# Expert blocks of 160, 128, 96 and 64 places with 32-wide halves, in a mixed order of experts, the loop written out

## The chip, the core and the metric

One core of one Trainium2 chip runs the program. The metric is the device time in microseconds of one execution, from three executions of each kernel: here their median. The engines are TensorE (PE; its weight loads are listed apart as PEld), VectorE (DVE), ScalarE (ACT), GpSimd (POOL) and SyncE (SP), which issues most of the transfers. All compute engines run their instructions in the order of the program and wait on semaphores.

## What is computed

One decoder layer over 512 prompt tokens and 8 sample tokens: modulation, a first norm, a combined projection into three mixers (pooling, convolution, gated recurrence), an output projection, and then a mixture of experts. The change touches the mixture alone, cut here to its core (float32 throughout):

```python
logits = xt @ router_w + router_b                      # 520 tokens, 32 experts
top_v, top_i = lax.top_k(logits, 4); top_w = softmax(top_v)
# for each expert e, the rows of xt that chose it:
g = minimum(xblk @ w_gate[e] + b_gate[e], 7)
u = clip(xblk @ w_up[e] + b_up[e], -7, 7)
y = ((u + 1) * g * sigmoid(1.702 * g)) @ w_down[e] + b_down[e]
# each token: sum of its 4 rows y, weighted by top_w
```

Each of the three matrices of an expert is 1024 x 1024, 4 MB; the 32 experts hold 402.7 MB of weights, and each is read once. The tokens of these inputs fall on the experts unevenly: experts 0 and 1 get 85 and 46 rows, the other 30, sorted, get 146, 146, 120, 102, 101, 101, 90, 83, 66, 60, 60, and the rest 59 and fewer (counted from the reference's routing). 2080 rows in all.

## The kernel before

**Blocks.** Experts are handled in order of a rank: experts 0 and 1 have the ranks 0 and 1 whatever their load (their weights can be fetched before the routing is known), the others are ranked by load, computed on the device. A rank has a fixed number of places, in blocks of 64: two blocks for the ranks 0 and 1, three for 2 and 3, two for 4 to 11, one for 12 to 31, 46 blocks in all. Places that are not taken are skipped by the gathers and scatters, but are multiplied like the others. Rows beyond an expert's places go to `extras`, 24 optional passes after the loop; with these inputs none is taken, but PE still steps over them (17.2 us after its last product).

**Products.** A block of 64 rows is the stationary operand (128 x 64), the weights stream: `project` and `down` send, for each of the 8 pieces k of the contraction and each block, two matmuls (h = 0, 1) of 512 columns to the two halves of the array's columns; each float32 matmul is two MATMUL instructions in the trace, so there are 32 for one block and one matrix. `project(0, ...)` is the gate matrix, `project(1, ...)` the up matrix; both begin with a bias matmul per block (`btab`, `sel`, L1804). `turn_act` turns the activations of the blocks (four 128 x 128 transposes for each, L1499), `turn_rows` turns gathered rows (eight transposes).

**A stage `cycle(s, i)`** is on PE: gate and up of expert s, turns of rows for a coming expert, `down` of expert s - 1, `turn_act` of expert s. ACT evicts the gates (`gated`), the turned rows (`x_low`), the outputs of s - 1 (`y_rows`, L943) and then the turned activations aT of s (`a_turned`, L949); DVE clips (`clipped`), multiplies (`activate`), evicts the other half of turned rows (`x_high`, L1430) and makes `sel`. `down` of a stage waits for the aT of the stage before (`aT_a`), after gate and up are done.

**Order.** The first 11 stages (`PRE`) are written out: ranks 0, 1, 4, 2, 12, 13, 14, 3, 15, 16, 17; then `REP` = 7 rounds of a loop with three stages of 2, 1 and 1 blocks (`BLOCKS`, `RANKS`, `G_BANKS`, `TURNS` hold the tables).

**Weights.** SP fetches chunks of 1 MB into 18 buffers (`NBUF`); four chunks are one matrix, 384 chunks in all. Chunk n waits until PE has used chunk n - 18 (`m_used`). The first 12 are fetched before the routing is done. POOL issues the gathers of rows (`gather`) and the scatters of outputs (`scatter`), each after a copy of its 128 indices into a small tile (`index`, L611). `sunit` and `gidx` are the index tables that DVE makes just before the stage 0.

Of the kernel before, what the change touches and what calls it, by code (L numbers as in the profile page):

```python
# [28 lines left out]
COLS = 24 + XTRA  # L29
# [17 lines left out]
RANK_STEP = (1, 2, 2)  # L47
G_BANKS = ((0, 1), (4, 5), (4, 5), (4, 5, 0), (1,), (1,), (1,), (4, 5, 0), (1,), (1,), (1,), (4, 5), (1,), (1,))
U_BANKS = ((2, 3), (0, 1), (0, 1), (1, 2, 3), (2,), (2,), (2,), (1, 2, 3), (2,), (2,), (2,), (0, 1), (2,), (2,))
D_BANKS = ((2, 3), (2, 3), (4, 5), (3, 0, 4), (3,), (3,), (4,), (3, 0, 4), (3,), (3,), (3,), (4, 5), (3,), (3,))  # L50
Y_BUFS = ((0, 1), (2, 3), (4, 0), (1, 2, 3), (4,), (0,), (1,), (2, 3, 4), (0,), (1,), (2,), (3, 0), (1,), (2,))

TURNS = {-1: ((0, 0, 0),), 0: ((1, 1, 1),), 1: ((0, 0, 6),), 2: ((1, 1, 2), (0, 2, 3)), 3: ((1, 0, 14),),
         4: ((0, 1, 4), (1, 2, 5)), 5: ((0, 0, 15),), 6: (), 7: ((1, 1, 7),), 8: ((0, 0, 16),), 9: (), 10: ((0, 0, 17),),
         11: ((1, 1, 8),), 12: (), 13: ((0, 0, 18),)}
NEXT_COL = {(0, 0): 6, (0, 6): 3, (0, 3): 4, (0, 4): 15, (0, 15): 16, (0, 16): 17, (0, 17): 18, (0, 18): 19,
            (1, 1): 2, (1, 2): 14, (1, 14): 5, (1, 5): 7, (1, 7): 8, (1, 8): 9}
# [12 lines left out]
def trunk_program(nc, x_prompt, x_sample, state_pool, state_conv, state_lru_conv, state_lru_h, c_prompt, c_sample,  # L70
# [8 lines left out]
    def place(start, *items):  # L79
# [78 lines left out]
    (xc, yst_b), M1 = place(W0, ("xc", [P, KC, 64], F32), ("yst_b", [P, 2, 512], F32))  # L158
    (xrow, raw2, sel, gidx, sidx, sunit, gcur0, gcur1, scur0, scur1, scur2, scur3, scur4), M2 = place(
        N0, ("xrow", [P, 2, D], F32), ("raw2", [P, NBUF - 12, CH], F32), ("sel", [P, P], F32R),  # L160
        ("gidx", [P, COLS], I32), ("sidx", [P, COLS], I32), ("sunit", [P, COLS, 2], I32), ("gcur0", [P, 1], I32),
        ("gcur1", [P, 1], I32), ("scur0", [P, 1], I32), ("scur1", [P, 1], I32), ("scur2", [P, 1], I32),
        ("scur3", [P, 1], I32), ("scur4", [P, 1], I32))
    gcur, scur, xt = (gcur0, gcur1), (scur0, scur1, scur2, scur3, scur4), (xa, xb, xc)
# [17 lines left out]
    with ctx:  # L182
# [52 lines left out]
        y_a, cur_done, cur_set = sem("y_a"), sem("cur_done"), sem("cur_set")  # L235
# [57 lines left out]
        def val(c, k, i):  # L293

            return c if i is None else i * k + c

        def first_chunk(s):

            return 12 * s - 4 if s else 0

        def gate_end(s, i):
            return val(first_chunk(s) + 4, 36, i)

        def up_end(s, i):
            return val(first_chunk(s) + 8, 36, i)

        def down_end(s, i):

            return val(first_chunk(s) + 12, 36, i)

        def blocks(s, i, back=0):

            return val(sum(BLOCKS[:s - back]), 4, i)

        def turns(s, i):

            return val(1 + sum(len(TURNS[t]) for t in range(s)), 2, i)

        def y_uses(s, b):

            before = sum(Y_BUFS[t].count(b) for t in range(min(s, PRE)))
            return before
# [3 lines left out]

        def tasks(eng, cycle):

            for s in range(PRE):
                cycle(s, None)  # L330
            with eng.Fori(0, REP) as i:
                for s in range(PRE, PRE + 3):
                    cycle(s, i)
# [24 lines left out]
        def _(sp):  # L358
# [67 lines left out]
            def expert(s, i):  # L426

                if s < 2:
                    return s
                r = RANKS[s]  # L430
                at_ = slice(r, r + 1) if i is None else bass.ds(i * RANK_STEP[s - PRE] + r, 1)
                return sp.value_load(task_i[0:1, at_], min_val=0, max_val=E - 1)

            def fetch(s, i, c, src):

                n = first_chunk(s) + c
                if i is None and n < 12:
# [4 lines left out]
                elif i is None and n < NBUF:  # L442
                    sp.wait_ge(tables_done, 1)
                else:
                    sp.wait_ge(m_used, val(n - NBUF + 1, 36, i))
                m_load(n % NBUF, src)

            kept = [None]

            def cycle(s, i):  # L450

                if s == 2:
                    sp.wait_ge(tables_done, 1)
                e = expert(s, i)
                for c in range(8):
                    fetch(s, i, c, rows_of((moe_w_gate, moe_w_up)[c // 4], e, c % 4))
                if s:
                    if s == PRE:
                        before = sp.value_load(task_i[0:1, bass.ds(i * 2 + RANKS[PRE - 1], 1)], min_val=0, max_val=E - 1)
                    else:  # L460
                        before = kept[0]
                    for c in range(4):
                        fetch(s, i, 8 + c, rows_of(moe_w_down, before, c))
                kept[0] = e

            tasks(sp, cycle)
            e_last = sp.value_load(task_i[0:1, E - 1:E], min_val=0, max_val=E - 1)
            for c in range(4):
                n = first_chunk(E) + c
                sp.wait_ge(m_used, n - NBUF + 1)  # L470
                m_load(n % NBUF, rows_of(moe_w_down, e_last, c))
# [21 lines left out]
            for b in range(5):  # L493
                total = 16 * (y_uses(PRE - 1, b) + REP * sum(Y_BUFS[t].count(b) for t in (PRE - 1, PRE, PRE + 1)))
                sp.wait_ge(y_out[b], n * 16 + (total + 16 * (b == 2)) if b < 2 else total + 16 * (b == 2))
# [19 lines left out]
        def _(g):  # L515
# [89 lines left out]
            h2_last, y_last = g.to_reg(TOK - 1), g.to_reg(TOK * K * 2 - 1)  # L605
            copies = [0]

            def index(dst, src, i, per):

                copies[0] += 1  # L610
                g.tensor_copy(dst[:, :], src).then_inc(cur_done, 1)  # L611
                g.wait_ge(cur_done, val(copies[0], per, i))
                g.sem_inc(cur_set, 1)

            def gather(b, col, i, per=6):

                at_ = slice(col, col + 1) if i is None else bass.ds(i + col, 1)
                index(gcur[b], gidx[:, at_], i, per)
                g.indirect_dma_start(
                    out=xrow[:, b, :], out_offset=None, in_=h2_d,  # L620
                    in_offset=bass.IndirectOffsetOnAxis(ap=gcur[b][:, 0:1], axis=0),
                    bounds_check=h2_last, oob_is_err=False).then_inc(x_rows[b], 16)

            def scatter(b, unit, i, per=6):

                if i is None:
                    src = sunit[:, unit // 2, unit % 2:unit % 2 + 1]
                else:
                    src = sunit[:, bass.ds(i + unit // 2, 1), unit % 2]
                index(scur[b], src, i, per)  # L630
                g.indirect_dma_start(  # L631
                    out=y_d, out_offset=bass.IndirectOffsetOnAxis(ap=scur[b][:, 0:1], axis=0), in_=yst(b),
                    in_offset=None, bounds_check=y_last, oob_is_err=False).then_inc(y_out[b], 16)

            def scatter_all(s, i, before):

                first = (0, 2, 12, 4, 28, 29, 30, 8, 31, 32, 33, 14, 34, 35)[s]
                for b in range(BLOCKS[s]):
                    g.wait_ge(y_a, val(before + b + 1, 4, i))
                    scatter(Y_BUFS[s][b], first + b, i)  # L640

            def cycle(s, i):
                n = 1 + sum(len(TURNS[t]) for t in range(s))
                for b, _, col in TURNS[s]:
                    n += 1
                    g.wait_ge(xt_ps, val(n, 2, i))
                    gather(b, NEXT_COL[b, col], i)
                if s == PRE:
                    g.wait_ge(y_a, val(sum(BLOCKS[:PRE]), 4, i))
                    scatter(Y_BUFS[PRE - 1][0], 33, i)  # L650
                elif s:
                    scatter_all(s - 1, i, sum(BLOCKS[:s - 1]))

            g.wait_ge(tables_done, 1)
            gather(0, 0, None)
            gather(1, 1, None)
            g.wait_ge(xt_ps, 1)
            gather(0, 6, None)
            tasks(g, cycle)
            all_blocks, all_turns = sum(BLOCKS[:PRE]) + 4 * REP, 1 + sum(len(TURNS[t]) for t in range(PRE)) + 2 * REP  # L660
# [1295 lines left out]
```

## Time and profile before

| | us |
|---|---|
| three runs | 1493.52, 1494.40, 1495.11 |
| median | 1494.40 |
| the profiled execution's own time | 1492.49 |
| its span, first to last instruction | 1490.6 |
| before the first expert's gate matmul | 348.7 |
| the 32 experts, to the end of PE's last product | 348.7 to 1409.4 |
| optional passes stepped over, sum of rows, last norm | 1409.4 to 1490.6 |
| PE matmul busy in the span | 1346.0 (90%) |
| ACT, DVE, POOL busy | 203.9, 288.1, 131.8 |
| HBM read | 473.9 MB |

Start and length in the rows below are us from the start of the span; "x64" is the number of instructions merged into the row, and what stands in brackets is the idle time before it and what ended it. PE's matmuls overlap in its pipeline, so the distance between the starts of two rows is what a piece costs, not its length.

### The profile page before, as it was taken

What the parts mean: (1) busy time and instruction counts of PE and PEld (TensorE: products, weight loads), DVE (VectorE), ACT (ScalarE), POOL (GpSimd) and SP (SyncE); (2) the same over time, 40 slices, a digit from 0 to 9 for tenths busy, and PEclk for the clock granted to TensorE, in tenths of its full rate; (3) what the DMA queues carried; (4) which work ended last, traced back from release to release, by engine and by line L of the source; (5) the groups of instructions that cost most, each with busy time, mean ns of one, the idle gap of its engine ahead of it and who ended that gap; (6) DMA issues with size and microseconds to landing.
All of it is one profiled execution on the core that took longest, in us unless ns stands there. A gap on an engine that the chain in (4) does not pass through costs nothing.

```text
span 1490.6 us, 18893 instructions
## 1 busy us (share of the span) xinstructions
PE 1346.0 (90%) x7387; PEld 591.5 (40%) x7387; DVE 288.1 (19%) x539; ACT 203.9 (14%) x348; POOL 131.8 (9%) x247
## 2 busy tenths in 40 slices
PE   2999869757999999999999999999999999999756
PEld 1868748542333333333333333333333333333211
DVE  1633684560000010010001000010000001000026
ACT  3515432200010010000100110000100100001011
POOL 2010030000011011000100100001000000000100
PEclk7799979857999999999999999999999999999966
DMA  9441593459787599999999999999999999999753
GB/s 319 145 144 63 193 354 117 175 218 336 254 293 273 197 328 363 418 356 413 390 417 416 417 418 418 419 417 417 417 418 419 416 416 418 417 418 416 307 195 117
DMA packets 112644, 486.91 MB, mean 327 GB/s; under 512 B 14643, under 2 KB 22842, under 8 KB 79286
## 3 DMA queue, kind: packets, MB, share of 16 engines
q1 hardware_dynamic: 99690, 461.15, 79.1%
q0 software_dynamic: 9824, 21.78, 4.0%
q10 hardware_dynamic: 3076, 3.22, 0.7%
q8 instruction: 40, 0.66, 0.2%
q14 instruction: 14, 0.11, 0.0%
HBM read 473.93 MB, written 19.08 MB: 331 GB/s over the span
## 4 chain that ended last, share of the span: by engine, by line
PE 77%; DMA 9%; DVE 6%; SPq 3%; issue 2%; ACTq 1%; ACT 1%; POOL 0%; DVEq 0%; POOLq 0%
PE psum L1812 40%; PE psum L1826 18%; DMA raw<-in_moe_w_down 5%; PE psum L1499 4%; SPq L424 3%; PE psum L1494 2%; PE psum L1495 2%; PE psum L1496 2%; PE psum L1804 2%; DMA bd_x<-in_lru_wx 1%; PE psum L1648 1%; ACTq L705 1%; DMA raw<-in_w_out 1%; PE psum L1926 1%; DVE acc L1472 1%
## 5 line engine op out<-in xcount | busy, mean ns | idle before, releaser
L1812 PE MATMUL psum<-raw,xa 128*64 128x512 f32 x1536 | 341.4, 597 | 1.0 <-DMA raw<-in_moe_w_up 1.0
L1826 PE MATMUL psum<-raw,aT 128*64 128x512 f32 x1472 | 324.9, 595 | 7.1 <-DMA raw<-in_moe_w_down 6.3
L1812 PE MATMUL psum<-raw,xb 128*64 128x512 f32 x1280 | 284.5, 595 | 0.0
L1416 DVE TENSOR_SCALAR act_t<-psum 128x512 f32<-128x512 f32 x46 | 30.5, 689 | 961.8 <-PE psum L1812 961.8
L1812 PEld LDWEIGHTS psum<-raw,xa 128*64 128x64 f32 x1536 | 106.4, 137 | 208.7 <-issue 204.0
L1826 PEld LDWEIGHTS psum<-raw,aT 128*64 128x64 f32 x1472 | 103.6, 137 | 209.6 <-issue 189.3
L1812 PEld LDWEIGHTS psum<-raw,xb 128*64 128x64 f32 x1280 | 90.2, 137 | 179.4 <-issue 179.4
L929 ACT ACTIVATE glu<-psum 128x512 f32<-128x512 f32 x46 | 25.9, 596 | 309.0 <-PE psum L1812 309.0
L1494 PE MATMUL psum<-hT_hi,w_hi 128*128 128x260 f32 x208 | 59.4, 286 | 0.0
L1495 PE MATMUL psum<-hT_lo,w_hi 128*128 128x260 f32 x208 | 58.8, 283 | 0.0
L1496 PE MATMUL psum<-hT_hi,w_lo 128*128 128x260 f32 x208 | 58.6, 282 | 0.0
L611 POOL COPY gcur<-gidx 128x1 int32<-128x1 int32 (+1 forms) x28 | 8.0, 287 | 556.1 <-PE psum L1499 511.5
L943 ACT ACTIVATE yst_a<-psum 128x512 f32<-128x512 f32 x32 | 18.9, 596 | 205.2 <-PE psum L1826 205.2
L1499 PE MATMUL psum<-ident,xrow 128*128 128x128 f32 x208 | 30.9, 293 | 15.5 <-DMA xrow<-h_scratch,gcur 11.9
L611 POOL COPY scur<-sunit 128x1 int32 (+1 forms) x46 | 8.5, 184 | 410.0 <-ACT yst_b L943 209.0
L1555 PE MATMUL psum<-raw,cT 128*9 128x128 f32 x768 | 32.3, 334 | 10.8 <-DMA raw<-in_ada_w 9.0
L1804 PE MATMUL psum<-btab,sel 128*128 128x512 f32 x92 | 38.8, 471 | 0.9 <-DVE xa L1430 0.9
L1499 PEld LDWEIGHTS psum<-ident,xrow 128*128 128x128 f32 x208 | 25.8, 195 | 34.6 <-issue 22.6
L1494 PEld LDWEIGHTS psum<-hT_hi,w_hi 128*128 128x128 f32 x208 | 39.1, 188 | 0.9 <-issue 0.8
L1496 PEld LDWEIGHTS psum<-hT_hi,w_lo 128*128 128x128 f32 x208 | 39.3, 189 | 0.0
L1495 PEld LDWEIGHTS psum<-hT_lo,w_hi 128*128 128x128 f32 x208 | 39.1, 188 | 0.1
L631 POOL DMA_INDIRECT y_scratch<-yst_a,scur x33 | 33.5, 1014 | 26.5 <-POOL scur L611 26.5
(368 smaller groups left out, 1013.7 us busy)
## 6 DMA issues: line engine op xcount, KB each, us to landing
raw<-in_moe_w_gate SPq DMA_DIRECT2D x128, 1024.0 KB, 19.1
raw<-in_moe_w_up SPq DMA_DIRECT2D x128, 1024.0 KB, 22.1
raw<-in_moe_w_down SPq DMA_DIRECT2D x128, 1024.0 KB, 23.4
raw<-in_ada_w SPq DMA_DIRECT2D x24, 1024.0 KB, 9.1
yrow<-y_scratch SPq DMA_DIRECT2D x4, 2048.0 KB, 9.7
raw<-in_w_in SPq DMA_DIRECT2D x7, 1024.0 KB, 11.6
x<-in_x_prompt SPq DMA_DIRECT2D x2, 2048.0 KB
raw<-in_w_out SPq DMA_DIRECT2D x4, 1024.0 KB, 14.2
```

The lines of the kernel that those rows point to most:

```text
L424: sp.dma_start(buf(slot).rearrange("p (k n) -> p k n", k=2), src).then_inc(m_full[slot], 16)
L631: g.indirect_dma_start(out=y_d, out_offset=bass.IndirectOffsetOnAxis(ap=scur[b][:, 0:1], axis=0), in_=yst(b), in_offset=None, bounds_check ...
L929: ac.activation(glu[:, b, :], bk[bank], ACT.Gelu_apprx_sigmoid).then_inc(glu_done, 1)
L1416: v.tensor_scalar(act_t[:, b, :], bk[bank], 8.0, -6.0, ALU.min, ALU.max).then_inc(u_done, 1)
L1494: mm(out, lhi, rhi, start=start, stop=False)
L1495: mm(out, lhi, rlo, start=False, stop=False)
L1496: return mm(out, llo, rhi, start=False, stop=stop)
L1499: return nc.tensor.transpose(out, src, ident[0:rows, 0:rows])
L1555: last = mm(outs[j], cT[:, 4 * kh + k, :], raw[:, slot, 512 * k + P * j:512 * k + P * j + P], start=False, stop=(kh == 1 and k == 3))
L1804: mm(bk[bank], sel[:, :], btab[:, mat, :], start=True, stop=False)
L1812: last = mm(bk[bank][64 * h:64 * h + 64, :], x[:, 2 * j + kk, at_:at_ + 64], buf(slot)[:, w:w + 512], start=False, stop=(j == 3 and kk == 1))
L1826: last = mm(bk[bank][64 * h:64 * h + 64, :], aT[:, b, k % 4, 64 * (k // 4):64 * (k // 4) + 64], buf(slot)[:, w:w + 512], start=(k == 0), s ...
```

## The change

1. **Places.** Units of 32: rank 0 and 1 get 96 places, 2 and 3 get 160, 4 to 7 get 128, 8 to 12 get 96, the others 64 (`width_of` counts units of 32). That is 38 blocks of 64 and 9 of 32. With the loads above no expert overflows.
2. **Half blocks.** `products` gives a block of 32 rows four matmuls of 256 columns, one to each quarter of the array's columns; the output takes 256 columns of a bank, and its evictions on ACT and DVE are 128 x 256. Its bias is four float32 matmuls of 256 columns. It is turned by two transposes. Half blocks stand behind the full blocks of their expert within each k.
3. **Order.** `ORDER` mixes the ranks; all 32 stages are written out on every engine, no `Fori`. The order has runs of single blocks: two behind each expert of 128 places at first, then five stages of 96 in a row, later six single blocks (stages 22 to 27) between the two experts of 160.
4. **Banks.** New tables; the turned activations of a third block go to bank 4. PE now waits for `aT_a` (all turned activations so far evicted) at the top of each stage, ahead of the gate's bias; `down` no longer waits for it.
5. **Gathers and scatters.** `gather` takes only the rows needed (96, 32 or 128), straight from `gidx`; scatters read `sunit` or, for half blocks, the new table `qunit`. The copies of indices are gone from the 32 stages. There are 25 gathers and turns of rows where there were 28 and 26; no stage has two turns (two had). `sunit` and `qunit` are made behind `tables_done` (4 and 8 small operations of DVE), no longer ahead of it.

```diff
-BLOCKS = (2, 2, 2, 3, 1, 1, 1, 3, 1, 1, 1, 2, 1, 1)
-RANKS = (0, 1, 4, 2, 12, 13, 14, 3, 15, 16, 17, 5, 18, 19)
-PRE, REP = 11, 7
+ORDER = (0, 1, 13, 14, 4, 15, 16, 5, 17, 18, 6, 8, 9, 10, 11, 12, 7, 19, 20, 21, 22, 2, 23, 24, 25, 26, 27, 28, 3, 29, 30, 31)
+def width_of(rank):
+    return 2 + (rank < 13) + (rank < 8) + (rank < 4) - 2 * (rank < 2)
+BLOCKS = {2: (64,), 3: (64, 32), 4: (64, 64), 5: (64, 64, 32)}
+G_BANKS = {2: (0,), 3: (0, 1), 4: (0, 1), 5: (0, 1, 3)}
+U_BANKS = {2: (1,), 3: (5, 4), 4: (4, 5), 5: (4, 5, 2)}
+T_BANKS = (6, 7, 4)
...
-    index(gcur[b], gidx[:, at_], i, per)
-    g.indirect_dma_start(
-        out=xrow[:, b, :], out_offset=None, in_=h2_d,
+def gather(n):
+    col, rows, _ = GATHERS[n]
+    rows_from(xrow[0:rows, n % 2, :], gidx[0:rows, col:col + 1], rows, x_rows[n % 2])
...
 for h in range(2):
     for a in range(2):
-        link(v.tensor_scalar(sunit[...], ...))          # ahead of tables_done
+        link(v.tensor_scalar(sunit[...], ...))          # behind tables_done
+for a in range(2):
+    for q in range(4):
+        link(v.tensor_scalar(qunit[32 * q:32 * q + 32, :, a], idx_f[64 * a:64 * a + 32, 0:15], 4.0, float(q),
...
+def bias(out, mat, w):
+    if w == 64:
+        mm(out, sel[:, :], btab[:, mat, :], start=True, stop=False)
+    else:
+        for g4 in range(4):
+            h, c = g4 // 2, 256 * (g4 % 2)
+            mm(out[32 * g4:32 * g4 + 32, :], sel[:, 64 * h:64 * h + 32].bitcast(F32),
+               btab[:, mat, c:c + 256].bitcast(F32), start=True, stop=False)
+def products(out, w, x, k, weights, start, stop):
+    for g4 in range(128 // w):
+        last = mm(out[w * g4:w * g4 + w, :], x[g4], weights[:, 8 * w * g4:8 * w * g4 + 8 * w],
+                  start=start, stop=stop)
...
 pe.wait_ge(xg_d, ...)
+if s:
+    pe.wait_ge(aT_a, before)
 project(0, ...)
...
-    pe.wait_ge(aT_a, val(before, 4, i))
     down(...)
```

How it stands on PE inside the gate matrix of an expert of more than two blocks. Before, rank 2 (`raw_164` is the second group of weight buffers, xb and xc the turned rows of its blocks 1, 2 and 3):

```order
L1812 MATMUL psum<-raw_164,xb 64x512 [waits m_full14]
L1812 MATMUL psum<-raw_164,xb 64x512 x3
L1812 MATMUL psum<-raw_164,xc 64x512 x2
L1812 MATMUL psum<-raw_164,xb 64x512 x4
L1812 MATMUL psum<-raw_164,xc 64x512 x2
```

And in the changed kernel, in the first stage (rank 0, one block of 64 and one of 32):

```order
L1812 MATMUL psum<-raw,xb 64x512 [waits m_full0]
L1812 MATMUL psum<-raw,xb 64x512
L1812 MATMUL psum<-raw,xb 32x256 x4
L1812 MATMUL psum<-raw,xb 64x512 x2
L1812 MATMUL psum<-raw,xb 32x256 x4
```

Before, all products have the one shape 64x512; now the shape goes from 64x512 to 32x256 and back at each k of the stages with a half block.

On PE at the border between two stages, where the turned activations of one expert are followed by the bias of the next; before:

```order
L1499 MATMUL psum<-ident,act_t 128x128 [waits xg_d,xg_a,act_done]
L1499 MATMUL psum<-ident,act_t 128x128 x11
L1804 MATMUL psum<-btab,sel 128x512 [waits xg_d,y_a,xg_a,sel_done]
L1812 MATMUL psum<-raw,xa 64x512 [waits m_full8]
```

and now, behind rank 2 as before:

```order
L1497 MATMUL psum<-ident,act_t 128x128 [waits xg_d,xg_a,act_done]
L1497 MATMUL psum<-ident,act_t 128x128 x9
L1802 MATMUL psum<-btab,sel 128x512 [waits aT_a,xg_d,y_a,xg_a,sel_done]
L1812 MATMUL psum<-raw,xa 64x512 [waits m_full8]
```

The bias has one semaphore more, `aT_a`, and there are 10 transposes where there were 12.

## Rows read from the trace of the kernel before

**Rows 1.** The page: GB/s that the DMA engines moved, 40 slices of 37.3 us.

```profile
GB/s 319 145 144 63 193 354 117 175 218 336 254 293 273 197 328 363 418 356 413 390 417 416 417 418 418 419 417 417 417 418 419 416 416 418 417 418 416 307 195 117
```

**Rows 2.** Windows: us, busy time of PE, PEld, DVE, ACT, POOL, clock, DMA share, GB/s.

```profile
757.78:1119.50 361.72, 361.72 (x1698) 126.98 (x1697) 27.51 (x52) 31.18 (x57) 30.84 (x48) 1.00 1.02 418
1119.50:1409.50 290.00, 281.81 (x1307) 97.20 (x1305) 20.64 (x39) 24.33 (x44) 24.33 (x38) 1.00 0.99 404
```

**Rows 3.** Waits of PE, 330 to 1435 us: total us, times, longest us.

```profile
PE psum L1826 <- DMA raw<-in_moe_w_down: 6.3, 10, 1.3
PE psum L1499 <- DVE xb L1430: 6.0, 3, 2.4
```

**Rows 4.** The chain of waits: one-block stages and the starts of the loop's last rounds.

```profile
1029.81 13.88 PE psum L1812 x64
...
1120.25 13.88 PE psum L1812 x64
...
1148.69 1.09 PE psum L1499 x8
...
1158.06 7.02 PE psum L1812 x32
...
1213.38 13.88 PE psum L1812 x64
```

**Rows 5.** The chain of waits over the whole span: the end.

```profile
1307.00 13.88 PE psum L1812 x64
...
1409.45 17.23 issue
```

**Rows 6.** Timeline of PE: a stage border of two-block experts.

```profile
414.79 13.95 PE L1826 MATMUL psum<-raw,aT 128*64 128x512 f32 x64
428.67 1.09 PE L1499 MATMUL psum<-ident,act_t 128*128 128x128 f32 x8
429.52 0.72 PE L1804 MATMUL psum<-btab,sel 128*128 128x512 f32 x2
430.17 13.95 PE L1812 MATMUL psum<-raw,xa 128*64 128x512 f32 x64
```

**Rows 7.** Timeline of PE: two steps k apart in the three-block expert.

```profile
480.59 1.03 PE L1812 MATMUL psum<-raw,xc 128*64 128x512 f32 x4
...
483.16 1.03 PE L1812 MATMUL psum<-raw,xc 128*64 128x512 f32 x4
```

**Rows 8.** Timeline of PE: the sample rows' output projection, four column groups of 256.

```profile
272.55 0.62 PE L1727 MATMUL psum<-w_hi,oS 128*8 128x256 f32 x8
...
279.02 0.61 PE L1727 MATMUL psum<-w_lo,oS 128*8 128x256 f32 x8
279.57 0.63 PE L1750 MATMUL psum<-rw,h2T 128*128 128x32 f32 x4
```

**Rows 9.** Windows over those groups (columns as in rows 2).

```profile
272.55:279.02 6.47, 6.47 (x121) 3.30 (x124) 3.01 (x4) 2.95 (x7) 0.53 (x1) 1.00 0.21 84
```

**Rows 10.** Timeline of all engines at a border between single blocks.

```profile
1029.10 0.71 PE L1804 MATMUL psum<-btab,sel 128*128 128x512 f32 x2
1029.38 0.60 ACT L949 ACTIVATE aT<-psum 128x512 f32<-128x512 f32 x1
```

**Rows 11.** Timeline: ACT at the border of rows 6.

```profile
429.76 1.09 ACT L949 ACTIVATE aT<-psum 128x512 f32<-128x512 f32 x2
```

**Rows 12.** Timeline: the last aT eviction and the product that waits for it.

```profile
1399.86 0.60 ACT L949 ACTIVATE aT<-psum 128x512 f32<-128x512 f32 x1
...
1400.55 3.65 PE L1826 MATMUL psum<-raw,aT 128*64 128x512 f32 x16 [0.73 <-ACT aT L949]
```

**Rows 13.** Timeline: from the tables to the first gather.

```profile
333.67 0.84 DVE L1398 TENSOR_SCALAR sunit<-idx_f 64x48 int32<-64x48 f32 x4
...
334.79 0.31 POOL L611 COPY gcur<-gidx 128x1 int32<-128x1 int32 x1 [44.54 <-DVE gidx L1403]
336.01 1.09 POOL L619 DMA_INDIRECT xrow<-h_scratch,gcur  x1 [0.92 <-POOL gcur L611]
```

More of the change, by code:

```diff
@@ new lines, in plan_turns @@
+def plan_turns():
+    made, turns = set(), [[] for _ in range(E + 1)]
+    for s, r in enumerate(ORDER):
+        col = unit_of(r) // 2
+        if col not in made:
+            made.add(col)
+            rows = {2: P, 3: 96, 4: P, 5: P}[WIDTH[s]]
+            turns[s].append((col, rows, 0 if WIDTH[s] == 2 else 1))
+        if WIDTH[s] == 5:
+            turns[s - 1].append((col + 1, 32, 2))
+    flat = [(s - 1, t) for s in range(E + 1) for t in turns[s]]
+    return [[(n,) + t for n, (c, t) in enumerate(flat) if c == s - 1] for s in range(E + 1)], [t for _, t in flat]
@@ L291, in buf, with gate_end, up_end, down_end @@
             return raw[:, n, :] if n < 12 else raw2[:, n - 12, :]
-        def val(c, k, i):
-            return c if i is None else i * k + c
         def first_chunk(s):
             return 12 * s - 4 if s else 0
[L301 to L322, printed above, removed]
+        def gate_end(s):
+            return first_chunk(s) + 4
+        def up_end(s):
+            return first_chunk(s) + 8
+        def down_end(s):
+            return first_chunk(s) + 12
+        def bank_of(banks, s, b):
+            w = BLOCKS[WIDTH[s]][b]
+            return bk[banks[WIDTH[s]][b]][:, 0:8 * w]
+        def down_bank(s, b):
+            w = BLOCKS[WIDTH[s]][b]
+            banks = D_EARLY if s < E - 1 and WIDTH[s + 1] == 5 else D_BANKS[WIDTH[s]]
+            return bk[banks[b]][:, 0:8 * w]
+        def y_uses(b):
+            return len(range(b, ALL_BLOCKS, Y_BUFS))
         def yst(b):
             return yst_a[:, b, :] if b < 3 else yst_b[:, b - 3, :]
[L327 to L333, printed above, removed]
         def extras(eng, cycle):
@@ new lines, in _, with index @@
+            g.wait_ge(tables_done, 1)
+            gather(0)
+            gather(1)
+            g.wait_ge(xt_ps, 1)
+            gather(2)
+            g.wait_ge(units_done, 1)
+            for s in range(E):
+                for n, _, _, _ in TURNS[s + 1]:
+                    g.wait_ge(xt_ps, n + 1)
+                    if n + 2 < ALL_TURNS:
+                        gather(n + 2)
+                if s:
+                    scatter(s - 1)
+            scatter(E - 1)
+            def index(dst, src, at_, q):
@@ L624, in scatter @@
[L624 to L660, printed above, removed]
[L661 to L664 removed]
             def extra(q):
[L668 to L670 removed]
+                g.wait_ge(xt_ps, q + ALL_TURNS)
@@ new lines, in a_turned @@
+            def a_turned(blocks, before, q=None):
+                for b, w in enumerate(blocks):
+                    act.wait_ge(at_ps, before + b + 1 if q is None else q * 2 + (before + b + 1))
+                    ac.activation(aT[:, b, 0:w // 16, :].rearrange("p a b -> p (a b)"), bk[T_BANKS[b]][:, 0:8 * w], ACT.Copy)\
+                        .then_inc(aT_a, 1)
+            act.wait_ge(tables_done, 1)
+            x_low(xb, GATHERS[0][1], 1)
+            for s in range(E):
+                gated(gate_end(s), [bank_of(G_BANKS, s, b) for b in range(len(BLOCKS[WIDTH[s]]))])
+                for n, _, rows, x in TURNS[s + 1]:
+                    x_low(xt[x], rows, n + 1)
+                if s:
+                    y_rows(s - 1)
+                a_turned(BLOCKS[WIDTH[s]], blocks_before(s))
@@ L1797, in turn_rows, with project @@
                 for k in range(KC):
-                    last = turn(bk[6 + k // 4][:, (k % 4) * P:(k % 4) * P + P], xrow[:, b, k:D:KC], P)
+                    last = turn(bk[6 + k // 4][:, (k % 4) * P:(k % 4) * P + rows], xrow[0:rows, b, k:D:KC], rows)
                 last.then_inc(xt_ps, 1)
-            def project(mat, banks, parts, slot0, full):
-                for bank in banks:
-                    mm(bk[bank], sel[:, :], btab[:, mat, :], start=True, stop=False)
+            def bias(out, mat, w):
+                if w == 64:
+                    mm(out, sel[:, :], btab[:, mat, :], start=True, stop=False)
+                else:
+                    for g4 in range(4):
[6 more added lines that the diff above has]
+                              start=start, stop=stop)
+                return last
+            def project(mat, outs, widths, parts, slot0, full):
+                for out, w in zip(outs, widths):
+                    bias(out, mat, w)
                 for j in range(4):
@@ L1808, in project, with down @@
                     for kk in range(2):
-                        for bank, (x, at_) in zip(banks, parts):
-                            for h in range(2):
-                                w = D * kk + 512 * h
-                                last = mm(bk[bank][64 * h:64 * h + 64, :], x[:, 2 * j + kk, at_:at_ + 64],
-                                          buf(slot)[:, w:w + 512], start=False, stop=(j == 3 and kk == 1))
+                        for out, w, (x, at_) in zip(outs, widths, parts):
+                            last = products(out, w, [x[:, 2 * j + kk, at_:at_ + w]] * 4, 2 * j + kk,
+                                            buf(slot)[:, D * kk:D * kk + D], False, j == 3 and kk == 1)
                     last.then_inc(m_used, 1)
-            def down(banks, slot0, full):
+            def down(outs, widths, slot0, full):
                 for j in range(4):
@@ L1857, in cycle @@
                 if s >= 3:
-                    pe.wait_ge(y_a, blocks(s, i, 2))
-                project(0, G_BANKS[s], parts_of(s), c0, full(0))
+                    pe.wait_ge(y_a, blocks_before(s - 2))
+                project(0, [bank_of(G_BANKS, s, b) for b in range(len(widths))], widths, parts_of(s), c0, full_at(c0))
                 if s >= 2:
-                    pe.wait_ge(y_a, blocks(s, i, 1))
-                project(1, U_BANKS[s], parts_of(s), c0 + 4, full(4))
-                n = 1 + sum(len(TURNS[t]) for t in range(s))
@@ L1864, in cycle @@
-                for b, _, _ in TURNS[s]:
-                    rows[0][b] += 1
-                    turn_rows(b, val(16 * rows[0][b], 16, i), val(before, 4, i) if before else None, val(n, 2, i))
-                    n += 1
-                if s:
-                    pe.wait_ge(glu_done, val(before + BLOCKS[s], 4, i))
-                    pe.wait_ge(aT_a, val(before, 4, i))
-                    down(D_BANKS[s - 1], c0 + 8, full(8))
-                pe.wait_ge(act_done, val(before + BLOCKS[s], 4, i))
@@ new lines, in _ @@
+                for n, _, rows, _ in TURNS[s + 1]:
+                    turn_rows(n % 2, rows, 16 * (n // 2 + 1), before if before else None, n)
+                if s:
+                    pe.wait_ge(glu_done, before + len(widths))
+                    down([down_bank(s - 1, b) for b in range(len(BLOCKS[WIDTH[s - 1]]))], BLOCKS[WIDTH[s - 1]],
+                         c0 + 8, full_at(c0 + 8))
+                pe.wait_ge(act_done, before + len(widths))
+                pe.wait_ge(xg_a, turns_before(s + 1))
@@ L1883, in _ @@
+                pe.wait_ge(xg_d, turns_before(s + 1))
+                turn_act(widths)
+            pe.wait_ge(y_a, ALL_BLOCKS - 1)
+            pe.wait_ge(aT_a, ALL_BLOCKS)
             c0 = first_chunk(E)
-            down((3,), c0, lambda j: 16 * ((c0 + j) // NBUF + 1))
+            down([down_bank(E - 1, 0)], (64,), c0, full_at(c0))
             def extra(q):
```

338 lines of the change are left out of this document (152 added, 186 removed).

## The prediction

> **What bounds the kernel now.** I read the expert part, 348.7 to 1409.4 us, in the windows first. From 758 to 1120 us PE is busy for all of 361.7 us at the full clock, and the DMA share is 1.02 at 418 GB/s [rows 2]: both look full, so the busy shares don't decide. The chain of waits does: three rounds of the loop start 90.44 us apart (1029.81, 1120.25) and consist of PE work alone, then the distance grows to 93.13 and 93.62 us [rows 4, 5], with waits for chunks of `down` [rows 3]. So PE sets the pace almost to the end, and the fetches run ahead of it by up to 18 chunks. That lead is spent only in the last quarter: 36 chunks of 1.05 MB in 90.44 us are already 417 GB/s, and rows and outputs come on top. Earlier, the bandwidth is not used (175 to 363 GB/s in slices 8 to 16 [rows 1]), because experts of two and three blocks hold the buffers. A better order can win back only what PE lost to chunks. I put that at 2.7 + 3.2 us for the two long rounds and 5.2 us at the end: from 1307.00, one undisturbed round less its last turn and bias (1.1), plus the last `down` (7.0) and its wait for aT (0.9), ends at 1404.2 instead of 1409.4. In all **11.1 us**. Everything else must come out of PE's own work.
>
> **The change on PE, part by part.** The unit: one block and one matrix cost 7.02 us alone (L1812 x32) [rows 4] and two cost 13.88 [rows 6]; three blocks repeat a step k every 2.57 us [rows 7], 0.858 for each. So one block more is 6.87 us for a matrix, 20.6 us for three.
> - 46 full blocks become 38: 8 x 20.6 = **-164.9**.
> - 9 half blocks make 9 x 24 = 216 steps. Their form, four column groups of 256 float32 columns, stands in the trace: 15 groups of eight instructions from 272.55 to 279.02, 0.431 us each, at the full clock [rows 8, 9]. It is half a full block's 0.858, so four groups do run side by side. 216 x 0.431 = **+93.1**.
> - The shape changes twice in each of these steps. What a change costs: a `down` of 32 pairs needs 16 x 0.858 = 13.73 us, but its successor starts 13.88 behind it [rows 6]: 0.15 for one leaving and one entering, of which the starts of the single instructions give 0.10 to the pipe that runs empty and 0.05 to the weight load that was not pulled ahead. Behind the four-group stream it is 279.57 - 279.02 - 0.43 = 0.12 [rows 8]. Leaving 64-wide 0.10, entering 32-wide 0.03 (between 0.01 and 0.05, by columns loaded), leaving 32-wide 0.12, entering 64-wide 0.05: 0.29 a step, 0.27 to 0.32. 216 x 0.292 = **+63.1** (58 to 69). No row shows 64 to 32; every other change of width between busy stretches of this trace (128 to 64 and back, 128 to 32 and back; rows 6 and 8 stand for them) costs it, and I take the same.
> - Biases: 16 of 0.32 go ((430.17 - 429.52) / 2 [rows 6]), 18 of half blocks come at 0.43 + 0.12 + 0.02: -5.1 + 10.2 = **+5.1**.
> - Turns: 14 transposes of 0.109 less, -1.5; one turn of rows less, -1.1 (L1499 x8) [rows 4]. Two of the three waits for DVE behind a second turn go, -3.6 of the 6.0 [rows 3]; the first, of stage 0, stays. **-6.2**.
>
> Without the new wait that is -9.8: the half blocks save nearly nothing, since a step of 0.723 us replaces one of 0.858.
>
> **The new wait.** `aT_a` now stands ahead of the gate's bias, and PE has nothing behind it that may pass: gate and up of the next expert (14 us or more) queue there. Between single blocks the bias starts at 1029.10 and the aT eviction ends at 1029.98 [rows 10]: 0.88 us of new idle time. Between two-block experts the bias starts at 429.52 and ACT ends at 430.85, since it first evicts two outputs: 1.33 [rows 6, 11]. All of it was hidden under the gate. In the new order 12 of the 31 borders are single behind single (0.88), 6 are larger experts behind single or nothing (0.94), 7 follow a 96 (1.10), 4 follow a 128 (1.29), 2 follow a 160 (1.54): 32.2 us. From ACT's end to PE's start it takes 0.09 more (1400.46 to 1400.55 [rows 12]), 2.8. **+35.0**; the ends are 31 x 0.97 = 30 and 31 x 1.42 = 44. I take the composition, as each class has its row or lies between two.
>
> **Start.** Four `sunit` operations (0.84) leave the path and so does the index copy (1.22 from 334.79 to 336.01) [rows 13]: **-2.0**; the gather of 96 rows lands as that of 128 did. The rest of POOL's changes is hidden: gathers are issued two turns ahead, over 40 us. The end from 1409 on stays, with the 17.2 us of stepping [rows 5].
>
> **Chunks.** PE's sum so far is +23.2, so PE is slower and the fetches, which need 1 MB / 418 GB/s = 2.51 us a chunk, wait for it more than before. Single blocks drain the lead: 12 chunks (30.1) and their share of the 2080 rows of 8 KB (0.5 MB, 1.3) are 31.4 us of fetching, against 23.3 of PE (3 x 7.02, two biases, four transposes, 1.0 of border) or 24.4 with a turn. In the run of six singles, the first of which has the `down` of an expert of 160, that is five times 7.5, or 38 of the lead's 45 us (18 chunks); before it, experts of 96 and 128 fill it up. So the 11.1 us of waits go: **-11.1**.
>
> **Sum.** -164.9 + 93.1 + 63.1 + 5.1 - 6.2 + 35.0 - 2.0 - 11.1 = **+12.1**. The profiled execution took 1492.49 us (1.9 below the median of the three), and would take 1504.6; the median goes from 1494.4 to **1506.5**.
>
> **A rule against the rows.** The rows show empty-pipe gaps only where 128 is one of the two widths. The Trainium skill (TensorEngine Tiling (Array Packing), Key Properties) says that a change of tiling mode, not of the tile, drains TensorE, and lists 64 and 32 columns as different modes; by that rule the +63.1 stands. Its page TensorE: Matmul & The Clock Gate (Part 3, The mechanism) speaks against the change altogether: a weight load overlaps running matmuls only where its row group differs, and here all four column groups share their rows. Rows 9 speak against that for this form: 124 loads, busy 3.30 us, lie inside 6.47 us in which PE is busy throughout.
>
> **Rivals.**
> 1. *No drain between 64 and 32.* Both are column groups, and only leaving them might empty the pipe. Then the 63.1 and 2.2 of the biases go: -53 against before. The fetches become the bound in the runs of singles and give back 3 to 10, so about **1448** (1444 to 1456). For: no row shows this pair. Against: every other pair pays. Chance 0.15.
> 2. *The lead runs dry.* In the six singles the margin is 7 us at 418 GB/s. At the 404 of the last window [rows 2] a single costs 1.1 us more, and the lead may not be full behind the 160. Then 5 to 15 us of chunk waits stay: **1517** (1512 to 1524). This decides from about 9 us of shortfall a single. Chance 0.08.
> 3. *Weight loads are not hidden in the half blocks.* With 32 columns loaded in place of 8, 3.30 / 15 = 0.22 us a step would come bare: +47, **1554**. It is what the second rule above would make of rows 9. Chance 0.03.
> 4. *Smaller prices.* If the border waits sit at their low end (-5) and a fifth to a third of the drains is covered by the loads (-12 to -21), the time is 1480 to 1490. Chance 0.07.
>
> **How the numbers follow.** My forecast, all terms as priced, has 0.67; its own range from the bounds of drains, waits and biases is 1497 to 1516. With rival 2, the upper part of rival 4 and half-hits between them, 1488 to 1522 holds 8 in 10; the case without drains is left out below. A measurement of this kernel can tell 0.2% (3 us) from no change. Faster by more: rival 1, and most of 4, 0.20. Within: 0.04. Slower: 0.76.
>
> **What will show it.** In the changed trace: (a) 32x256 products in groups of eight 0.43 us long, and the next 64-wide start about 0.55 after the group's first, a step of 96 places taking 1.58 us (1.29 if nothing drains); (b) a new PE wait for ACT's aT at the bias, 31 times, near 1.0 us each; (c) chunk waits near nothing; (d) a single's stage 23.3 us without a turn; (e) the last product ending near 1421. The forecast is wrong if (a) shows 1.29, or if (b) is missing.

## The result, and the profile after

The changed kernel takes 1505.82 us (median of four runs, 1503.76 to 1508.16) against 1494.14 us (four runs, 1493.52 to 1495.11): a ratio of 1.009 with a 95% interval of 1.0066 to 1.0114, 11.7 us slower. Forecast were 1506.5 us and +12.1 us.

The page of the changed kernel (its profiled execution took 1508.16 us, the slowest of the four): busy time of TensorE and of its weight loads, and the DMA row in GB/s that answers to [rows 1].

```profile
span 1506.4 us, 20098 instructions
...
PE 1334.8 (89%) x8453; PEld 549.9 (37%) x8453; DVE 284.3 (19%) x548; ACT 199.1 (13%) x350; POOL 111.7 (7%) x171
...
GB/s 321 146 136 49 204 338 124 168 226 354 275 360 417 416 419 416 399 410 406 371 299 312 304 306 311 301 413 416 418 416 394 404 416 416 417 419 416 302 167 116
```

TensorE is busy 11 us less (it was 1346.0) in a span 16 us longer. The fetches reach full bandwidth in slice 13 and not in slice 17, some 145 us earlier, but in slices 21 to 26, the five experts of 96 places, they fall to 300 GB/s, since TensorE frees the buffers too slowly there: such a stage takes 42.9 us (753.99 to 796.92), in which 12 chunks are 293 GB/s, and rows and outputs come on top. Where it stands idle, in the waits of TensorE from 330 to 1440 us (total us, times, longest):

```profile
PE psum L1802 <- ACT aT L960: 32.8, 31, 1.6
PE psum L1497 <- DMA xrow<-h_scratch,gidx: 10.8, 1, 10.8
PE psum L1497 <- DVE xb L1436: 1.8, 1, 1.8
...
```

The first row is the new wait, once at each of the 31 borders; the two rows left out are 0.7 us each. No wait for a chunk is left, where [rows 3] had 6.3 us for `down` alone. One matrix with a full and a half block, and the biases around it, in the timeline of TensorE (start, length; L1806 is the half block's bias):

```profile
753.99 0.47 PE L1802 MATMUL psum<-btab,sel 128*128 128x512 f32 x1 [1.35 <-ACT aT L960]
754.38 0.64 PE L1806 MATMUL psum<-btab,sel 128*32 128x256 f32 x8
754.95 12.70 PE L1812 MATMUL psum<-raw,xb 128*64 128x512 f32 x96
767.58 0.50 PE L1802 MATMUL psum<-btab,sel 128*128 128x512 f32 x1
```

From 754.95 to 767.58 are 12.63 us for eight steps, 1.58 us a step. Two full blocks took 13.88 us [rows 6], one takes 7.02 [rows 4]. So a block of half the rows costs 5.61 us of the 6.87 of a full one. In an expert of 160 places the timeline shows the two widths apart; a half block's eight products and the next two full ones:

```profile
1287.52 0.64 PE L1812 MATMUL psum<-raw,xc 128*32 128x256 f32 x8
1288.08 1.94 PE L1812 MATMUL psum<-raw,xb 128*64 128x512 f32 x8
```

The starts of the single instructions are those of the prediction: 0.523 us from the last 64-wide product to the first 32-wide one, 0.309 from the last 32-wide to the next 64-wide, each time 0.07 us ahead of the end of the last product before, 216 times the one way and 189 the other.

### The profile page after: what moved, and what is told of

It reads as the page before. It is cut to its first block, busy times and chain, and to the rows that moved or that the text cites. A ratio compares the mean times of both kernels' runs of the same rounds, so it can differ in the third digit from the quotient of the medians.

```text
span 1506.4 us, 20098 instructions
## 1 busy us (share of the span) xinstructions
PE 1334.8 (89%) x8453; PEld 549.9 (37%) x8453; DVE 284.3 (19%) x548; ACT 199.1 (13%) x350; POOL 111.7 (7%) x171
## 4 chain that ended last, share of the span: by engine, by line
PE 81%; DVE 6%; DMA 4%; ACT 4%; issue 3%; ACTq 1%; SPq 1%; POOL 0%; DVEq 0%
PE psum L1812 63%; PE psum L1497 3%; PE psum L1492 2%; PE psum L1493 2%; PE psum L1494 2%; PE psum L1802 2%; ACT aT L960 1%; DMA bd_x<-in_lru_wx 1%; PE psum L1646 1%; ACTq L715 1%; ACT yst_a L954 1%; DMA raw<-in_w_out 1%; DVE acc L1470 1%; PE psum L1806 1%; PE psum L1928 1%
## 5 line engine op out<-in xcount | busy, mean ns | idle before, releaser
L1812 PE MATMUL psum<-raw,xb 128*64 128x512 f32 (+1 forms) x2112 | 353.7, 517 | 0.0
L1812 PE MATMUL psum<-raw,aT 128*64 128x512 f32 (+1 forms) x1792 | 318.1, 532 | 0.7 <-ACT yst_a L954 0.7
L1812 PE MATMUL psum<-raw,xa 128*64 128x512 f32 x1216 | 269.3, 595 | 0.0
L1423 DVE TENSOR_SCALAR act_t<-psum 128x512 f32<-128x512 f32 (+1 forms) x47 | 28.7, 638 | 989.7 <-PE psum L1812 989.7
L1812 PEld LDWEIGHTS psum<-raw,xb 128*64 128x64 f32 (+1 forms) x2112 | 91.7, 124 | 242.4 <-issue 242.4
L1812 PEld LDWEIGHTS psum<-raw,aT 128*64 128x64 f32 (+1 forms) x1792 | 91.3, 127 | 211.3 <-issue 207.6
L625 POOL DMA_INDIRECT xrow<-h_scratch,gidx x25 | 28.9, 1155 | 568.6 <-PE psum L1497 524.1
L939 ACT ACTIVATE glu<-psum 128x512 f32<-128x512 f32 (+1 forms) x47 | 24.6, 556 | 349.3 <-PE psum L1812 349.3
L637 POOL DMA_INDIRECT y_scratch<-yst_a,sunit x25 | 24.8, 994 | 375.9 <-ACT yst_a L954 328.2
L1553 PE MATMUL psum<-raw,cT 128*9 128x128 f32 x768 | 31.3, 326 | 11.4 <-DMA raw<-in_ada_w 10.2
L1497 PE MATMUL psum<-ident,xrow 128*128 128x128 f32 (+2 forms) x200 | 28.9, 289 | 10.8 <-DMA xrow<-h_scratch,gidx 10.8
## 6 DMA issues: line engine op xcount, KB each, us to landing
raw<-in_w_out SPq DMA_DIRECT2D x4, 1024.0 KB, 14.1
```

The lines of the kernel that those rows point to most:

```text
L625: g.indirect_dma_start(out=out, out_offset=None, in_=h2_d, in_offset=bass.IndirectOffsetOnAxis(ap=index, axis=0), bounds_check=h2_last, oo ...
L637: g.indirect_dma_start(out=out, out_offset=bass.IndirectOffsetOnAxis(ap=index, axis=0), in_=src, in_offset=None, bounds_check=last, oob_is ...
L939: ac.activation(glu[:, b, 0:bank.shape[1]], bank, ACT.Gelu_apprx_sigmoid).then_inc(glu_done, 1)
L1423: v.tensor_scalar(act_t[:, b, 0:bank.shape[1]], bank, 8.0, -6.0, ALU.min, ALU.max).then_inc(u_done, 1)
L1497: return nc.tensor.transpose(out, src, ident[0:rows, 0:rows])
L1553: last = mm(outs[j], cT[:, 4 * kh + k, :], raw[:, slot, 512 * k + P * j:512 * k + P * j + P], start=False, stop=(kh == 1 and k == 3))
```

## Where the 15 us of the expert part went

The expert part, from the first bias to the last product's end, is 1061.9 us before and 1077.1 us after. The distance from each TensorE instruction's start to the next one's, summed by what the instruction does, gives:

| | before | after | difference | forecast |
|---|---|---|---|---|
| products with chunk waits | 973.5 | 826.6 + 123.4 | -23.5 | -8.7 - 11.1 = -19.8 |
| biases | 34.3 | 29.6 + 10.8 | +6.1 | +5.1 |
| turns of rows and activations | 54.1 | 46.3 | -7.8 | -6.2 |
| held up at the borders by aT | 0.1 | 40.4 | +40.3 | +35.0 |
| sum | 1061.9 | 1077.1 | +15.2 | +14.1 |

Outside it: the first bias follows the sample rows' projection by 73.7 us where it was 75.0, so the start brought 1.3 us and not 2.0 (73.6 to 74.5 in the eight experiments with the new start, so rather 1). The profiled execution after was 4 us late already at that projection, at 276.7 us and not 272.5, ahead of every changed instruction. With 15.2 us of the expert part, 1.3 less of the start and 2.2 less behind the last product, these 4.1 us make the 15.8 us by which its span is longer, while the medians lie 11.7 apart.

## The experiments

All leave the computation whole, and differ from the named kernel in the lines shown.

### The wait, moved behind the gate

```diff
-if s:
-    pe.wait_ge(aT_a, before)
 project(0, ...)
+if s:
+    pe.wait_ge(aT_a, before)
 if s >= 2:
     pe.wait_ge(y_a, blocks_before(s - 1))
 project(1, ...)
```

The turned activations share banks only with the up matrix and later work, so the wait can stand there.

> The changed kernel with its one new wait moved: TensorE waits for the evicted aT ahead of the up matrix's bias, not ahead of the gate's; all else as changed. Theory (the border waits cost about 1.06 us at each of 31 borders, 32.8 us in the changed kernel's trace, and were hidden under the gate before): these go, chunk waits come back for 5 to 12 us, since TensorE is faster: 1477 us (1472 to 1484), faster than the kernel before. Rival (the wait only takes time that TensorE would have lost to something else, such as the drained pipe or the fetches): 1500 us or more.

Measured: 1482.98 us (1479.15 to 1485.18), 0.9919 of the kernel before (0.9898 to 0.9941). The waits of TensorE in the expert part:

```profile
PE psum L1812 <- DMA raw<-in_moe_w_down: 3.7, 6, 1.3
PE psum L1812 <- DMA raw<-in_moe_w_up: 2.8, 5, 0.6
PE psum L1812 <- DMA raw<-in_moe_w_gate: 2.0, 3, 1.1
```

The row of aT is gone, and chunks take 8.5 us of idle time. They cost more than that: the five matrices of single blocks in which they fall are 11.9 us longer than five undisturbed ones of 7.02. The border sum falls from 40.4 to 0.1 us and the expert part from 1077.1 to 1050.1; the stretch behind the last product is 5 us longer, which is why the whole gains 22.8 us and not 27. One line, moved by one matrix, is the difference between a kernel that is slower than the one before and one that is faster.

### The wait, added to the kernel before

```diff
 pe.wait_ge(xg_d, turns(s, i))
+if before:
+    pe.wait_ge(aT_a, val(before, 4, i))
 if s >= 3:
```

> The kernel before with only the new wait added: TensorE waits for all evicted aT ahead of each gate. Theory: 31 x 1.09 us of idle time, less the 11 us that the kernel before loses to chunks and would no longer: 1494 + 35 + 3 - 11 = 1520 us (1515 to 1526). Rival (the time is hidden by the fetches, whose share is 1.02 in the steady part): 1494 to 1500 us.

Measured: 1518.89 us (1518.18 to 1521.16), 1.017 of the kernel before (1.0153 to 1.0187). The timeline of all engines at a border behind a single block, as in [rows 10]:

```profile
1057.37 0.60 ACT L949 ACTIVATE aT<-psum 128x512 f32<-128x512 f32 x1
...
1058.10 0.72 PE L1804 MATMUL psum<-btab,sel 128*128 128x512 f32 x2 [0.77 <-ACT aT L949]
```

The bias starts 0.13 us behind the eviction's end (1057.97), where it started 0.88 us ahead of it [rows 10]: 1.01 us in all. The release takes 0.13 us here, but 0.25 at 22 of the 31 borders. The border sum is 40.6 us, and no chunk is waited for. What that is worth stands in the timeline of the kernel before. One of its six matrices with a chunk wait:

```profile
1389.97 1.94 PE L1826 MATMUL psum<-raw,aT 128*64 128x512 f32 x8
...
1399.16 0.66 PE L1499 MATMUL psum<-ident,act_t 128*128 128x128 f32 x4
```

It takes 9.19 us in place of 7.02, and 1.50 of the 2.17 more are idle time, in three waits. The other five (from 1202.55, 1287.74, 1296.72, 1381.19 and 1400.55) take 9.70, 7.89, 9.15, 7.69 and 8.90 us: 10.4 us more in all six. The products fall by 7.6 us only, from 973.5 to 965.9, because this execution also lost 2.9 us to TensorE's clock: 1.15 us in the first matrix of the second expert (15.67 us where it was 14.52), at whose start the clock stood at half speed for longer, and 1.70 in one of the sixth, a single block's, over which the window is

```profile
585.89:594.60 8.71, 8.71 (x33) 2.60 (x32) 0.00 (x0) 0.00 (x0) 2.35 (x4) 0.80 0.87 322
```

with 8.71 us in place of 7.02 and a granted clock of 0.80 in the mean: it stood at 0.5 (1.2 GHz) for 3.4 us from 586.9 and at full speed before and after. So the price of the wait is 40 us, 10.4 us of chunk waits pay a part back, and the stretch behind the last product is 5.8 us shorter (not explained, see below). The window over one steady round is

```profile
963.96:1058.10 94.14, 91.15 (x425) 31.80 (x425) 6.88 (x13) 7.80 (x14) 7.71 (x12) 1.00 1.02 418
```

The DMA share stays at 1.02, and still the time is lost: a busy share of 1.02 did not mean that the fetches were the bound.

### Half blocks by chunk, and by matrix

```diff
 pe.wait_ge(m_full[slot], full(j))
-for kk in range(2):
-    for out, w, (x, at_) in zip(outs, widths, parts):
-        last = products(...)
+for wide in (64, 32):
+    for kk in range(2):
+        for out, w, (x, at_) in zip(outs, widths, parts):
+            if w == wide:
+                last = products(...)
 last.then_inc(m_used, 1)
```

The same is done in `down`.

> The changed kernel with another order of products: within each chunk (two steps k) first the full blocks of both steps, then the half block's of both, so the width of the column groups changes twice in a chunk and not twice in a step: 108 round trips in place of 216, same products. The wait stays at the gate. Theory (a round trip costs 0.29 us whatever stands between): 108 x 0.29 = -31.5: 1474 us (1470 to 1480). Rival (the gaps belong to the half blocks' own groups, for instance to their weight loads, and not to the change of width): no change, 1506 us.

Measured: 1477.84 us (1472.86 to 1479.32), 0.9881 (0.9859 to 0.9903). The timeline of TensorE in stage 1:

```profile
393.53 11.54 PE L1812 MATMUL psum<-raw,xb 128*64 128x512 f32 x96
405.00 1.16 PE L1497 MATMUL psum<-ident,xrow 128*128 128x128 f32 x8
```

The same 96 instructions take 11.47 us, not 12.63: four round trips between the widths less, 0.29 us each. The border wait is still there (32.6 us of idle time).

> Both edits: the wait ahead of the up matrix and the half blocks grouped by chunk. Theory: -33 and -31.5 for TensorE, of which the fetches give back some 11 to 19 us as waits for chunks, in the runs of single blocks: 1450 us (1446 to 1458). Rival (the fetches already bind once one of the two is gone): no faster than the better of the two alone, about 1472 us.

Measured: 1452.38 us (1452.16 to 1456.87), 0.9731 (0.9712 to 0.975). The two edits add up: 22.8 and 28.0 us alone, 53.4 together. With both, TensorE waits 10.9 us for chunks (14.1 us by the length of the matrices), little more than the 8.5 (11.9) with the first alone.

For whole matrices the loop over the widths goes outside the loop over chunks, and `m_used` is counted in the last pass:

```diff
-for j in range(4):
-    slot = (slot0 + j) % NBUF
-    pe.wait_ge(m_full[slot], full(j))
+for wide in ((64, 32) if 32 in widths else (64,)):
+    for j in range(4):
+        slot = (slot0 + j) % NBUF
+        if wide == 64:
+            pe.wait_ge(m_full[slot], full(j))
...
+        if wide == min(widths):
+            last.then_inc(m_used, 1)
```

`down` is changed likewise, and the wait for aT stands ahead of the up matrix.

> The wait ahead of the up matrix, and the half blocks grouped by whole matrix: first the full blocks of all eight steps, then the half block's of all eight, with the chunks released only in the second pass. 27 changes of width and back in place of 216. Theory: against the version grouped by chunk (1452 us) TensorE saves 81 x 0.29 = 24 us more, but the chunks are released up to 10 us later and the fetches give back some 10: 1437 us (1434 to 1446). Rival (the fetches bind already, since they need 31.4 us an expert, 1005 us in all): 1450 us, no gain over the version grouped by chunk.

Measured: 1442.69 us (1440.19 to 1446.58), 0.9653 (0.9628 to 0.9677). The timeline of TensorE in stage 1:

```profile
391.96 10.68 PE L1812 MATMUL psum<-raw,xb 128*64 128x512 f32 x96
402.56 1.16 PE L1497 MATMUL psum<-ident,xrow 128*128 128x128 f32 x8
```

10.60 us: seven round trips less than in the changed kernel save 2.03 us, again 0.29 each. Three points (eight, four and one per matrix) lie on one line, so the price belongs to the change of width, not to the half block's own loads; its own cost is 7.02 + 8 x 0.431 = 10.47 us, and 10.60 with one entry. Of the 24 us that TensorE saves against the version by chunk, 14.7 shorten the expert part (1021.5 to 1006.8) and 10 the whole; the waits for chunks rise from 10.9 to 16.7 us of idle time, or from 14.1 to 22.6 us by the length of the matrices, near the 10 expected, and the stretch behind the last product is longer (below).

### Half blocks made full

```diff
 def width_of(rank):
-    return 2 + (rank < 13) + (rank < 8) + (rank < 4) - 2 * (rank < 2)
+    w = 2 + (rank < 13) + (rank < 8) + (rank < 4) - 2 * (rank < 2)
+    return 4 if w == 3 else w
```

> The changed kernel with the seven half blocks of the 96-place experts made full blocks of 64 (those experts get two full blocks, their places stay 96 in the tables); the two 160-place experts keep theirs. Theory (a half block's step costs 0.431 + 0.292 = 0.723 us against 0.858, and its biases more): 7 x 24 x 0.135 = 22.7 us more, 3.5 us less for the biases, 1.5 more for transposes: 1506 + 21 = 1527 us (1522 to 1532). Rival (as the streams alone say, 0.431 against 0.858): 1578 us. Rival (no gain in a half block at all): 1506 us.

Measured: 1533.02 us (1531.83 to 1536.94), 1.0267 (1.0245 to 1.029): 27 us more than the changed kernel, where 21 were expected. Both rivals are out. The miss is the same as in the table above: the expectation took 0.723 us for a half block's step and 12.80 for the matrix. It is 12.63, so that a full block costs 1.25 us more and not 1.08, 26.3 us in 21 matrices against the 22.7 taken. The products rose by 29.7 us in all. The other 3.4 are TensorE's clock in this one execution, which stood at 0.5 twice for 3.4 us, in two matrices of a single block:

```profile
1189.22:1197.93 8.71, 8.71 (x33) 2.61 (x32) 0.00 (x0) 0.00 (x0) 1.62 (x2) 0.80 0.83 316
```

The other, from 1400.47 us, has the same 8.71 us and 0.80.

### The order of the experts

```diff
-ORDER = (0, 1, 13, 14, 4, 15, 16, 5, 17, 18, 6, 8, 9, 10, 11, 12, 7, 19, ...)
+ORDER = (0, 1, 4, 13, 14, 2, 15, 16, 3, 17, 18, 5, 19, 20, 6, 21, 22, 7, 23, ...)
```

> The changed kernel with another order of experts alone, near that of the kernel before: each larger expert is followed by one or two single blocks (0, 1, 4, 13, 14, 2, 15, 16, 3, 17, 18, 5, 19, 20, ...). Same products, same half blocks, same wait at the gate. Theory (TensorE is the bound everywhere, the fetches have slack): no change, 1506 us (1503 to 1510). Rival (the mixed order is worth something by itself): above 1510 us.

Measured: 1506.58 us (1506.42 to 1506.84), 1.008 (1.0063 to 1.0097). No chunk is waited for with either order. The mixed order as such brings nothing where TensorE is the bound.

```diff
+ORDER = (0, 1, 13, 2, 14, 3, 15, 4, 5, 6, 7, 8, 9, 10, 11, 12, 16, 17, ..., 31)
```

> The changed kernel with the experts sorted: all larger ones first, then 16 single blocks in a row. Theory (a single block needs 31.4 us of fetching and 23.3 to 24.4 us of TensorE, and the lead is 45 us): the lead is gone after six, and the others cost the fetches' time, some 82 to 91 us in all: 1591 us (1585 to 1600). Rival (order does nothing as long as the sum of TensorE's work is the same): 1506 us.

Measured: 1590.46 us in one run. The windows of 100 us in it (us, busy time of PE, PEld, DVE, ACT, POOL, clock, DMA share, GB/s):

```profile
1100.00:1200.00 100.00, 92.11 (x418) 30.46 (x414) 7.17 (x14) 8.28 (x14) 6.16 (x6) 1.00 1.02 417
1200.00:1300.00 100.00, 79.99 (x342) 23.49 (x344) 7.16 (x14) 6.51 (x11) 5.16 (x5) 1.00 1.02 417
```

The DMA row reads the same in both, 1.02 and 417 GB/s; only TensorE's busy time shows that the lead has run out between them. The unbroken row of singles starts at 1033.4 us, and TensorE waits for a chunk for the first time at 1174.9, in the sixth. So the estimate of the lead (45 us, spent by about six singles) holds, and rival 2 of the prediction had its mechanism right and did not arise.

The last one puts such an order on the version grouped by matrix:

> The same with an order that spreads the larger experts so that the lead of the fetches is spent and filled up evenly (0, 1, 13, 14, 4, 15 to 18, 5, 8, 9, 10, 19, 11, 12, 6, 20, 21, 22, 2, 23 to 26, 7, 27, 28, 3, 29, 30, 31). Theory: the waits for chunks fall from about 21 us to 2 to 19 us: 1418 to 1435 us. Rival (the sum of the fetches is the bound, so order doesn't matter): same as with the order of the changed kernel.

Measured: 1434.60 us (1433.57 to 1440.76), **0.961 of the kernel before (0.9582 to 0.9637)**, 60 us less. The waits for chunks in it:

```profile
PE psum L1812 <- DMA raw<-in_moe_w_down: 7.6, 11, 2.5
PE psum L1812 <- DMA raw<-in_moe_w_up: 3.5, 7, 0.6
```

That is 11.1 us where the order of the changed kernel left 16.7 (7.7, 5.0 and 4.0). The medians are 8 us apart and the expert part 6.5 (1006.8 to 1000.3), but the two intervals just touch, so the gain of the order alone is likely and not certain. It is what one would look for where both sides are near their bound: from 600 to 900 us TensorE is busy for 298.3 of 300 us at a DMA share of 1.02. This is the fastest version that was run.

## Why the prediction was right

**TensorE as the bound.** Right. The chain of waits and the round lengths decided it, not the busy shares; the kernel before with 40 us more of TensorE's time got 25 us longer, with 10.4 us of chunk waits gone, and the sorted order shows what a real fetch bound looks like.

**Half blocks.** The form of [rows 8] came as priced: 0.431 us for eight instructions with 32 columns loaded as with 8. Rival 3 fell with it: the weight loads of the half blocks, whose column groups share their rows, are hidden. **The change of width**, 0.292 us for a round trip, was extended from 128-wide neighbours to 64 and 32; it measured 0.29 in three ways, so rival 1 is out, and the rule of the Trainium skill (TensorEngine Tiling (Array Packing), Key Properties), that a change of tiling mode drains the engine, holds here between two column widths. But I counted the 27 mixed matrices' own entry and exit (0.15 us) on top of eight round trips, although the eighth contains them: 12.80 us a matrix in place of 12.63. With the chunk waits apart, products fell by 13.1 us (973.5 - 10.4 to 950.0) and not by 8.7, and 27 times 0.17 make nearly all of these 4.4.

**The new wait.** Its mechanism was right, at 31 places; its size was too small. The evictions came nearly as composed (32.6 us for 32.2). For the release I took 0.09 us, from a product that waits for three semaphores [rows 12]. At the first two borders, where the bias does not wait for an output yet (three semaphores in the trace), it starts 0.14 us behind the eviction; at the other 29 it waits for five and starts 0.25 us or more behind it: 7.8 us in all and not 2.8. 40.3 us, not 35.0. Rival 4 had put this term lower, and it came higher. That the number of semaphores makes the difference fits these rows, but was not tried by itself, and at the starts of the loop's rounds in the kernel before with the wait it is 0.13.

**Chunks.** They went, as forecast, and were worth 10.4 us by the six matrices listed above, for 11.1 forecast: 2.7, 3.0 and 4.7 for the two long rounds and the end, where I had 2.7, 3.2 and 5.2.

**Biases, turns, start.** +6.1 for +5.1: the full ones fell by 4.7 us and not by 5.1, and those of the half blocks cost 10.8 and not 10.2. -7.8 for -6.2: turns of rows fell by 5.8 us, of which 4.2 are waits for DVE (6.0 to 1.8, where 2.4 were to stay), and turns of activations by 2.0. -1.3 for -2.0.

Of the signs named, the step of a half block (1.58 us), the 31 waits, the missing chunk waits and a single's stage of 23.3 us (1187.69 to 1210.96) came as forecast. The last product ends at 1427.5 and not near 1421: this execution was 4.1 us late before the first changed instruction, and the stretch behind the last product then gave 2.2 back.

Measured minus forecast, the terms are off by -4.4 (products), +5.3 (border), +0.7 (chunks), -1.6 (turns), +1.0 (biases) and +0.7 us (start), and the end by -2.2. They cancel: that the forecast of 12.1 us lies 0.4 us from the 11.7 measured is luck, since its terms are off by up to 5 us.

**Not explained.** The stretch behind the last product is not constant, as I had taken it: 81.2 us before, 79.0 after, 75.4 in the kernel before with the wait, 86.4 and 85.6 in the two fastest. In these the step over the optional passes leaves TensorE idle for 14.6 to 24.9 us [rows 5]. In the two fastest the last `down` waits for a chunk, but so it does in the kernel before, and with the wait moved behind the gate alone the stretch is 84.1 us without such a wait. The cause stays open.

## What to carry to other kernels

Count changes of the column-group width like instructions: with 0.29 us for a round trip, a half block that alternates with full ones within each 0.86 us step gives back two thirds of what it saves (0.858 - 0.431), and the same products in two passes keep nearly all of it. Put a wait at the last place that needs it: 0.6 us evictions that a 7 us matrix used to hide cost 40 us over 31 borders once the wait stood ahead of that matrix. When two resources both look full, read which one the round length follows, and how long the other's lead lasts; an order that mixes loads pays only once the faster side has become the bound.

## What the runs showed of the hardware that I had not expected

- The time from ScalarE's end to the start of the TensorE instruction that waits for it isn't one number: 0.09 us for a product and 0.14 for a bias that wait for three semaphores, 0.25 at most borders for a bias that waits for five.
- Four column groups of 32 loaded columns run at the rate of those with 8: 0.431 us for eight instructions of 256 float32 columns, and the gate and up matrices of an expert of 160 places, half block and all, run undisturbed with the DMA engines at 418 GB/s beside them (1285.7 to 1323.0 us in the changed kernel's trace).
- A DMA share of 1.02 and 417 GB/s stood in stretches with TensorE busy for 100%, 92% and 80% of the time.
- The granted clock fell to 0.5 for 3.4 us in the midst of the expert part, in some executions and not in others, at 1.70 us a time: at 586.9 us in the kernel before with the wait, at 1189.3 and 1401.0 us in the one with half blocks made full. Each time TensorE had stood idle for 1.6 to 1.8 us at the border just before; other borders of 1.6 us passed without it.
